# Splits of weight units moved from VectorE to GpSimd at nine seams, with VectorE's order changed at two of them

## The reference

```python
def first_block(x, ...):
    for l in range(2):
        p = x @ w_in[l]                                # 1024 -> 2304
        h = concat(gmlp, diff_attention, pool) @ w_out[l]
        x = layer_norm(ALPHA * x + h, ln1_g[l], ln1_b[l])
        f = swiglu(x, w1, w3, w2) if l == 0 else moe_ffn(x, router_w, ...)   # 2816; top 2 of 8 experts of 3584
        x = layer_norm(ALPHA * x + f, ln2_g[l], ln2_b[l])

def second_block(x, ...):
    for l in range(2):
        z = rmsnorm(x, norm_mix[l]) @ w_in[l]          # 1024 -> 6936
        merged = sum of three gated branches (sparse attention, retention, convolution)
        x = x + merged @ w_out[l]
        x = x + square(relu(rmsnorm(x, norm_mlp[l]) @ w_ff1[l])) @ w_ff2[l]
    return rmsnorm(x, norm_final)
```

## Time and profile before

| | us |
|---|---|
| median of 3 runs | 2530.76 (2528.2 to 2540.81) |
| the profiled execution's own time | 2539.47 |
| its span | 2537.6 |
| PE busy | 2456.3 (97%) |
| DVE busy | 1976.5 (78%) |
| ACT busy | 1472.9 (58%) |
| POOL busy | 32.3 (1%) |
| mean granted TensorE clock | 0.978 of full speed |

### The profile page before, as it was taken

The page is one execution under the profiler, slowest core; times in us unless marked ns, Lnnn a source line. Parts: engine busy times, 40 slices in busy tenths (PEclk is TensorE's granted clock), DMA queues, the critical chain, the costliest instruction groups (busy, mean ns, idle before and its releaser), DMA issues.

```text
span 2537.6 us, 29881 instructions
## 1 busy us (share of the span) xinstructions
PE 2456.3 (97%) x11624; PEld 2032.8 (80%) x11624; DVE 1976.5 (78%) x2452; ACT 1472.9 (58%) x1508; POOL 32.3 (1%) x44
## 2 busy tenths in 40 slices
PE   8999999899999999999999998999999999999998
PEld 6678877688888888888888886788778878877887
DVE  4855567899899989998989997878875667896655
ACT  4344442677777777777777775356444544644443
POOL 0000000000000000000000000000000000000000
PEclk9999998899999999999999998899999998999999
DMA  8366553699999999999999996543556674445664
GB/s 268 104 183 188 174 166 131 231 347 364 372 364 349 364 371 363 350 362 374 360 345 369 365 366 233 152 147 111 163 179 182 183 224 126 117 144 167 187 191 133
DMA packets 274156, 626.18 MB, mean 247 GB/s; under 512 B 17899, under 2 KB 27255, under 8 KB 273880
## 3 DMA queue, kind: packets, MB, share of 16 engines
q1 hardware_dynamic: 271708, 615.92, 71.4%
q0 software_dynamic: 1872, 6.82, 0.8%
q10 hardware_dynamic: 428, 1.45, 0.2%
HBM read 623.06 MB, written 1.07 MB: 246 GB/s over the span
## 4 chain that ended last, share of the span: by engine, by line
PE 85%; DVE 10%; ACT 3%; issue 1%; DMA 0%; POOL 0%; DVEq 0%; SPq 0%; POOLq 0%; ACTq 0%
PE tile L672 25%; PE tile L674 25%; PE tile L673 25%; PE aux L792 4%; DVE units_parts L1829 3%; DVE zbuf L2437 1%; PE aux L1042 1%; PE aux L1160 1%; ACT high L1378 1%; PE aux L965 0%; PE aux L1250 0%; DVE x_sb L1916 0%; DVE acts L1785 0%; DVE x_sb L1914 0%; DVE acc L1954 0%
## 5 line engine op out<-in xcount | busy, mean ns | idle before, releaser
L1829 DVE TENSOR_TENSOR units_parts<-units,high 128x1024 fp32r<-128x1024 f32 (+3 forms) x514 | 727.8, 1423 | 317.5 <-ACT high L1378 310.9
L1378 ACT ACTIVATE high<-units 128x1024 fp32r<-128x1024 f32 (+3 forms) x514 | 624.7, 1219 | 471.4 <-PE tile L674 427.1
L672 PE MATMUL tile<-high,acts 128*128 128x512 f32 (+2 forms) x1464 | 581.5, 397 | 18.3 <-DVE units_parts L1829 11.3
L673 PE MATMUL tile<-units_parts,acts 128*128 128x512 f32 (+1 forms) x1504 | 582.6, 387 | 0.0
L674 PE MATMUL tile<-high,acts 128*128 128x512 f32 (+2 forms) x1464 | 567.5, 388 | 0.0
L672 PEld LDWEIGHTS tile<-high,acts 128*128 128x128 f32 x1464 | 280.5, 192 | 78.5 <-DVE units_parts L1829 22.5
L673 PEld LDWEIGHTS tile<-units_parts,acts 128*128 128x128 f32 x1504 | 288.3, 192 | 52.5 <-issue 0.5
L674 PEld LDWEIGHTS tile<-high,acts 128*128 128x128 f32 x1464 | 279.6, 191 | 56.1
L674 PE MATMUL tile<-high,zbuf_parts 128*128 128x512 f32 x692 | 269.6, 390 | 0.0
L673 PE MATMUL tile<-units_parts,zbuf_parts 128*128 128x512 f32 x632 | 246.0, 389 | 0.0
L672 PE MATMUL tile<-high,zbuf_parts 128*128 128x512 f32 x596 | 234.0, 393 | 0.0
(11 more groups left out here) (377 smaller groups left out, 3939.4 us busy)
## 6 DMA issues: line engine op xcount, KB each, us to landing
units<-in_moe_w SPq DMA_DIRECT2D x216, 1024.0 KB, 5.5
units<-in_w_in SPq DMA_DIRECT2D x136, 512.0 KB, 3.8
units<-in_w_ff SPq DMA_DIRECT2D x128, 512.0 KB, 3.7
q_buf<-in_moe_w SPq DMA_DIRECT2D x54, 1024.0 KB, 5.4
k_buf<-in_moe_w SPq DMA_DIRECT2D x54, 1024.0 KB, 5.7
nat<-in_moe_w SPq DMA_DIRECT2D x54, 1024.0 KB, 5.4
units<-in_ffn_w SPq DMA_DIRECT2D x62, 512.0 KB, 4.3
units<-in_w_out SPq DMA_DIRECT2D x32, 512.0 KB, 3.5
```

Of the source, the lines that this page charges most:

```text
L672: nc.tensor.matmul(bank, lhs[0], high, start=start, stop=False)
L673: nc.tensor.matmul(bank, lhs[0], low, start=False, stop=False)
L1378: nc.scalar.activation(high_slot(SG[0], n) if wide_ else high_slot(SG[0], n)[:, 0:cols], halves(weights) if wide_ else weights[:, 0:cols], ...
L1829: V.tensor_tensor(low, weights, high, ALU.subtract).then_inc(SG[0].low_ready, 1)
```

## The change

Thirty-five splits go from VectorE to GpSimd: the first four units behind each of eight seams (the dense feed-forward of block 1, the input product of its layer 1, and in each layer of block 2 the input product, the output product and the feed-forward), and the first three units (of 2048 columns) of the experts. They have a semaphore of their own, `pool_low`, and TensorE waits for it or for `low_ready` by the unit's number. VectorE's `split` leaves them out.

- Block 1, norms 0 and 1: GpSimd makes the power of block 0, four splits, then the power of block 1.
- Norm 2 (in front of the router): VectorE adds both halves of block 1 and asks for its moments before it takes the low parts of block 0; GpSimd makes the three splits after both powers. ScalarE makes the high parts of two expert units before block 1's activations and the third before the router's exponential.
- Entry of block 2: VectorE scales block 0 before it takes block 1's moments; GpSimd makes three splits between the powers and one behind.
- Block 2: in front of the power for the root's factor, GpSimd makes the splits of the seam (or seams) before it.
- `x` is split within round 0, behind the third and fifth tile, and no longer in front of it.

```diff
+POOLED1 = firsts(SEAM_FF, SEAM_IN) + [SEAM_MOE + i for i in range(3)]
+POOLED2 = firsts(*[l * LAYER2 + n for l in range(DEPTH) for n in (0, SEAM_OUT2, SEAM_FF2)])
...
-                pe.wait_ge(SG[0].low_ready, n + 1)
+                by_pool = sum(m < n for m in pooled(SG[0]))
+                if n in pooled(SG[0]):
+                    pe.wait_ge(SG[0].pool_low, by_pool + 1)
+                else:
+                    pe.wait_ge(SG[0].low_ready, n - by_pool + 1)
...
                                 if r == 0:
-                                    pe.wait_ge(x_split, 1)
+                                    pe.wait_ge(x_split, TB)
...
-                    for b in range(TB):
-                        highs_block(True, 4, b)
+                    END[0] += EXPERT_LEAD
+                    highs_block(True, 4, 0)
+                    ahead(END[0] - 1)
+                    highs_block(True, 4, 1)
+                    ahead(END[0])
                     act.wait_ge(route_dif, 1)
                     nc.scalar.activation(small[:, 8:10], small[:, 0:2], ACT.Exp).then_inc(route_exp, 1)
-                    END[0] += EXPERT_LEAD
-                    ahead(END[0])
...
+            def by_block(first=None, units=0):
                 for b in range(TB):
                     power(1, b)
+                    if b == 0 and units:
+                        lows(S, first, units)
+
+            def lows(sig_, first, units):
+                for n in range(first, first + units):
+                    pool.wait_ge(sig_.high_ready, n + 1)
+                    weights, low, _, _ = slot(sig_, n)
+                    high = high_slot(sig_, n)
+                    if expert_unit(sig_, n) >= 0:
+                        weights, low = halves(weights), halves(low)
+                    nc.gpsimd.tensor_tensor(low, weights, high, ALU.subtract).then_inc(sig_.pool_low, 1)
...
+            power(1, 0)
+            lows(S2, 0, 3)
+            power(1, 1)
+            lows(S2, 3, 1)
+            load_gain(5)
             for l in range(DEPTH):
+                if l > 0:
+                    lows(S2, LAYER2, HIGHS)
                 power(TB)
...
                 power(TB * RET_H)
                 power(TB)
+                lows(S2, l * LAYER2 + SEAM_OUT2, HIGHS)
+                lows(S2, l * LAYER2 + SEAM_FF2, HIGHS)
                 power(TB)
...
                     n = C.split.take()
+                    if n in pooled(SG[0]):
+                        continue
...
-                half_in(0, 0)
-                add_half(1, 0, factor)
-                half_in(0, 1)
                 if between:
+                    for h in range(2):
+                        add_half(1, h, factor)
+                    sums_taken()
+                    second = ask_moments(1, x)
+                    block_in(0)
                     between()
-                add_half(1, 1, factor)
-                sums_taken()
-                second = ask_moments(1, x)
+                else:
+                    half_in(0, 0)
+                    add_half(1, 0, factor)
+                    half_in(0, 1)
+                    add_half(1, 1, factor)
+                    sums_taken()
+                    second = ask_moments(1, x)
```

More of the change, by code:

```diff
@@ L116, with after, firsts @@
 STREAM2 = DEPTH * (IN2 + BRANCH2 + OUT2 + FF2)
+def after(*stages):
+    return sum(map(len, stages))
+def firsts(*starts):
+    return [n + i for n in starts for i in range(HIGHS)]
+SEAM_FF, SEAM_IN, SEAM_MOE = after(IN1, OUT1), after(IN1, OUT1, FF1), after(STREAM1)
+SEAM_OUT2, SEAM_FF2, LAYER2 = after(IN2, BRANCH2), after(IN2, BRANCH2, OUT2), after(IN2, BRANCH2, OUT2, FF2)
+POOLED1 = firsts(SEAM_FF, SEAM_IN) + [SEAM_MOE + i for i in range(3)]
+POOLED2 = firsts(*[l * LAYER2 + n for l in range(DEPTH) for n in (0, SEAM_OUT2, SEAM_FF2)])
 class Tally:
@@ L136, in __init__ @@
         self.low_ready = sem("low_ready" + suffix)
+        self.pool_low = sem("pool_low" + suffix)
         self.unit_done = sem("unit_done" + suffix)
@@ L480, in row, with pooled @@
             return src.rearrange("(o n) -> o n", o=1).to_broadcast([P, width])
+        def pooled(sig_):
+            return POOLED1 if sig_ is S else POOLED2
         turned_at, scored_at, sums_at = {}, {}, []
@@ L1714, in power @@
                 nc.gpsimd.tensor_tensor(rs_out[:, at], rs_in[:, at], half[:, at], ALU.pow).then_inc(rstd_ready, 1)
-            def by_block():
+            def by_block(first=None, units=0):
                 for b in range(TB):
                     power(1, b)
+                    if b == 0 and units:
[8 more added lines that the diff above has]
+                    nc.gpsimd.tensor_tensor(low, weights, high, ALU.subtract).then_inc(sig_.pool_low, 1)
             load_gain(0)
@@ L1725, in _ @@
                 power(HEADS1, HEADS1)
-                by_block()
-                load_gain(2 * l + 1)
[L1728 to L1731, removed]
+                if l == 0:
+                    by_block(SEAM_FF, HIGHS)
+                else:
+                    by_block()
+                    lows(S, SEAM_MOE, 3)
+                load_gain(2 * l + 1)
+                if l == 0:
+                    by_block(SEAM_IN, HIGHS)
+                    load_gain(2)
+            load_gain(4)
+            power(1, 0)
[3 more added lines that the diff above has]
+            load_gain(5)
             for l in range(DEPTH):
+                if l > 0:
+                    lows(S2, LAYER2, HIGHS)
                 power(TB)
@@ L1931, in layer_norm @@
                 normal_block(0, x, first)
-                half_in(0, 0)
-                add_half(1, 0, factor)
-                half_in(0, 1)
                 if between:
-                    between()
-                add_half(1, 1, factor)
-                sums_taken()
-                second = ask_moments(1, x)
+                    for h in range(2):
[3 more added lines that the diff above has]
+                    block_in(0)
+                    between()
+                else:
+                    half_in(0, 0)
[4 more added lines that the diff above has]
+                    second = ask_moments(1, x)
                 next_units()
@@ L2355, in expert @@
                         hidden_low(t - 1)
+                    if r == 0 and t in (2, 4):
+                        b = t // 2 - 1
+                        dve.wait_ge(x_high_ready, b + 1)
+                        V.tensor_tensor(x_low[:, b, :], x[:, b, :], x_high[:, b, :], ALU.subtract).then_inc(x_split, 1)
                 if gathers(r):
@@ L2376, in _ @@
             find_extra()
[L2377 to L2380, removed]
             rounds(dve, expert, route_mask, extra)
@@ L2385, in _ @@
             gain_in(4)
[L2386 to L2390, removed]
+            add_back(0)
+            read_back()
+            answer = ask_moments(0, acc)
+            add_back(1)
+            read_back()
             V.memset(small[:, 21:22], 0.0).then_inc(params_used, 1)
-            normal_block(0, acc, answers[0], 4)
-            next_units(2)
+            normal_block(0, acc, answer, 4)
+            answer = ask_moments(1, acc)
             block_in(0)
+            normal_block(1, acc, answer, 4)
             next_units()
-            normal_block(1, acc, answers[1], 4)
             block_in(1)
```

## The result

| | before | after |
|---|---|---|
| median of 12 runs, us | 2530.95 (2528.2 to 2540.81) | 2547.79 (2542.0 to 2553.99) |
| ratio, 95% interval | | 1.0061 (1.0045 to 1.0077) |
| profiled execution's own time, us | 2539.47 | 2546.14 |
| its span, us | 2537.6 | 2544.4 |

The change makes the kernel 16.8 us slower by the medians, and 0.6% by the ratio, with an interval of 0.45 to 0.77%. That is clear of no change; the 0.5% at which the prediction draws the line between same and slower lies inside the interval. The forecast was 2554, the range 2512 to 2566.

The account below looks back on a forecast made before the run. TensorE, busy 97% of the span, was taken as the bound, so only its standstills at the seams could change. Terms 6.6 + 5.6 + 3.3 + 4.4 + 3.3 = +23.2 us on the median 2530.76 gave 2554, range 2512 to 2566.

Parts of the forecast that it names:

- What a split costs on GpSimd: A GpSimd split was taken as 2.2 us for 1024 columns and 4.0 for 2048, from memset and power times.
- Mutual hold-up: Likeliest case: VectorE instructions reading two SBUF tensors and GpSimd's splits each wait for the other; +23.2 us, chance 0.50.
- Rival 1: Both engines run freely, since VectorE does not wait for GpSimd, and the splits hide: -16.2 us, 2514.5, chance 0.27.
- rival 2: VectorE always goes first and its two-tensor work stretches GpSimd's splits: -5 us, 2526, chance 0.23.
- Norms 0 and 1: Three splits slip between block 0's four scaling instructions, and block 1 waits less: +3.3 us at each norm, +6.6 together.
- Norm 2: Splits delay block 1's scaling by 6.5 us and a VectorE subtraction by 2.0; TensorE's 2.9 us wait goes: +5.6.
- Entry of block 2: Splits hold the scaling of both blocks, and block 1's ends at 1599.7 instead of 1596.4: +3.3 us.
- `x`'s split within round 0: 2.4 us move from the front of round 0 into VectorE's queue within it, covered by its lead: 0.
- Output seams: In block 2, VectorE's two sums of token block 1 meet the second and third splits: +2.2 us each, +4.4 together.
- Feed-forward and input seams: In block 2, block 1's scaling ends 1.4 us later, less 0.3: +1.1 us at each of three seams, +3.3 together.
- the working's own two points: Sum of the mutual-waiting case by GpSimd split time: +23.2 us at 2.2 us a split, +31 at 2.6.
- put the step on the median: The +23.2 us was added to the median 2530.76, not to the profiled execution's 2539.47, giving 2554 instead of 2562.7.

Follow-up runs that it names:

- e3: The changed kernel with each GpSimd split cut into four instructions of a quarter of the columns: 2547.91 us, ratio to before 1.0061.
- e9: The changed kernel with the three expert splits back on VectorE, in the changed order, the other 32 on GpSimd: 2539.45 us, ratio to before 1.0035.
- e7: The changed kernel with the splits of norms 0 and 1 back on VectorE, the other 27 on GpSimd: 2542.22 us, ratio to before 1.0040.
- e6: The kernel before, with no edit, run again for a second profile: 2527.84 us.

## Why the prediction was right, and where its sizes were off

The forecast's side and mechanism held, and the time was 6 us too high.

- **What a split costs on GpSimd.** 2.2 and 4.0 us predicted, 2.38 and 4.50 measured. At 1024 columns this is near by luck, since two errors pull against each other: 0.74 us for 256 columns (e3), 2.38 for 1024 and 4.50 for 2048 make 2.1 ns a column and 0.2 us fixed, where the working had 1.7 ns and 0.55 us. The figure of the Trainium skill (GPSIMD Engine Reference, § Elementwise — side-by-side cycle accounting), 4.5 us for 2048 columns of `tensor_tensor`, is what the trace has (4.50).
- **Mutual hold-up** is shown: by the three scaling instructions, by their going back to 0.75 us in e9, and by e3, where the hold shrank with the piece. Rival 1 (free running) and rival 2 (GpSimd gives way) fall by the same rows: L1966 took 2.80 and 4.55 us. GpSimd is held too: 2.6 us a split between VectorE's instructions, 2.38 alone.
- **Norms 0 and 1**: +3.3 each predicted, +3.4 measured; e7 agrees in the medians. The parts fit less well than the total. A hold was shorter than a split, 2.0 to 2.1 us, three of them 6.1 for the 6.6 predicted, so block 0 was scaled 4.3 us later and not 4.7. VectorE then waited 0.71 us for ScalarE's high part of block 0, where it had waited 0.16 before, and that made up the difference. The row of before:

```profile
128.09 0.69 DVE L1785 TENSOR_TENSOR acts<-aux,acts 128x512 fp32r<-128x512 f32 x1 [0.16 <-ACT acts L1409]
```

- **Norm 2**: +5.6 predicted, +5.1 measured. Its parts: scaling +6.7 (6.5), L2296 +2.4 (2.0), the gather at half clock +0.6 (not foreseen), the front of round 0 -4.5 (-2.9). The last was more than the wait: in the kernel before the clock was low after that wait, as the windows of before and of after show. Against e6, where it was low for longer, this part is -6.0 and the seam +3.7.

```profile
476.00:480.00 4.00, 2.53 (x6) 2.05 (x7) 4.00 (x3) 0.67 (x1) 0.00 (x0) 0.63 0.80 295
```

```profile
476.00:480.00 4.00, 4.00 (x19) 3.28 (x18) 3.62 (x26) 2.08 (x2) 0.00 (x0) 1.00 0.23 45
```

- **Entry of block 2**: +3.3 predicted, +3.6 measured, with four holds of 1.5 to 2.0 us where the working had three splits and a fourth in the way.
- **`x`'s split within round 0**: 0 predicted and measured; the rounds keep their length to 0.03 us.
- **Output seams**: +2.2 each predicted, +0.35 measured. This is the term that was mis-sized. VectorE's second sum was held as foreseen, by 1.45 us; the rows are of after and then of before.

```profile
1858.81 2.15 DVE L2708 TENSOR_TENSOR acc<-acc,q_buf 128x512 f32<-128x512 f32 x1
```

```profile
1854.59 2.35 DVE L1829 TENSOR_TENSOR units_parts<-units,high 128x1024 fp32r<-128x1024 f32 x2
```

I took off "the 0.4 us by which the third unit's split was late", and forgot these two splits: they stood between the sums and block 1's low parts, and 2.35 us of VectorE's time went with them.
- **Feed-forward and input seams**: +1.1 each predicted, +0.6 measured, and by another wait: TensorE waited for GpSimd's splits, not for the scaling. TensorE's waits of after, 1875 to 1900 us, and then its wait for the scaling in before, 1870 to 1895 us, which is gone:

```profile
PE tile L697 <- POOL units_parts L1755: 1.4, 2, 1.1
```

```profile
PE aux L792 <- DVE nat L1947: 0.8, 1, 0.8
```

Block 1's last scaling there (L2005, which was L1947) was held by 1.46 us:

```profile
1883.85 2.15 DVE L2005 TENSOR_TENSOR nat<-x_sb,gain 128x512 f32<-128x512 f32 x1
```

The working has it end 1.4 us later than before. The products in front of the seam run 5.1 us later in this trace than in the first profile, and against them it ended 0.9 us earlier, at 1886.0 for 1881.8: here too the working kept the hold and left out the two splits that had gone from in front of it.

The sum of the seams was 17.9 where the working had 23.2: 3.7 of the difference lie in the output seams and 1.6 in the other three. With the measured 2.38 us a split, the working's own two points (+23.2 at 2.2 us, +31 at 2.6) would have given about +27, so the short price of a split hid a part of the excess. Its upper bound of 2566 does not follow from them either: +31 on the median is 2562; nothing turned on it. The choice to put the step on the median, and not on the profiled execution's own time, was right for a reason that I did not know then: that execution had the half-clock stretch at 382 to 405 us.

## What to carry to other kernels

An idle GpSimd is no free second VectorE. Before work moves there, list what VectorE executes in that stretch: beside sums from PSUM and moments two splits were free (-1.3 us a seam at norms 0 and 1), while beside instructions with two SBUF inputs each split held VectorE for 2 or 4 us on the critical chain, where VectorE makes the same split itself in 1.2 or 2.3. Whatever is wanted from GpSimd soon (here the power) must stand in front of the long pieces in its queue. And before two profiles are compared by their spans, compare the granted clock stretch by stretch; here one such stretch moved a profile by 7.5 us with no change in the program.

## What was not expected of the hardware

- Stretches of half clock come and go between executions of one program: 0.50 against 0.90 at 382 to 405 us.
- VectorE's cast of 128x16 and tensor-scalar of 128x8, with one tensor from SBUF, were held too (0.93 for 0.17, 2.67 for 0.63 in four). The Trainium skill (SBUF — State Buffer, § Who interferes with whom) counts copies, casts and tensor-scalar instructions among those that can take both of VectorE's read ports; the trace agrees.
- The smallest instruction waits for the end of a split like a large one: 2.57 us for 128x2, which took 0.16 before.
- GpSimd's splits do not cut up for free: 0.74 us for 256 columns, 2.38 for 1024, 4.50 for 2048.
